# A decoder trunk of eight layer norms in split float32: the shift matmul in float32r, 128-column statistics, and two ScalarE operations of the SwiGLU loop in another order

## The reference

```python
x = layer_norm(alpha * x + 0.5 * swiglu_a(x))
x = layer_norm(alpha * x + mixer_i(x))          # layer 0: windowed attention with sinks, layer 1: NSA
x = layer_norm(alpha * x + cross_attention(x, mem))
x = layer_norm(alpha * x + 0.5 * swiglu_b(x))

def swiglu(x, w_gate, w_up, w_down):            # 1024 -> 2816 -> 1024
    return (silu(x @ w_gate) * (x @ w_up)) @ w_down
def layer_norm(x, g, b):
    mu = mean(x); var = mean((x - mu) ** 2)
    return (x - mu) * rsqrt(var + 1e-5) * g + b
```

## Time and profile before

| what | us |
|---|---|
| median of 3 runs | 2193.94 |
| lowest, highest | 2190.92, 2194.06 |
| the profiled execution, its own time | 2193.49 |
| its span in the profile | 2191.7 |

### The profile page before, as it was taken

How to read it: one execution, slowest core, us unless ns; L and a number is a source line. 1 busy time by engine, 2 the same in 40 slices (tenths; PEclk the granted TensorE clock), 3 DMA queues, 4 the chain that set the end, 5 groups by cost and what they waited for, 6 DMA issues and landing times.

```text
span 2191.7 us, 35422 instructions
## 1 busy us (share of the span) xinstructions
PE 2170.3 (99%) x13654; PEld 1923.6 (88%) x13654; DVE 1334.5 (61%) x2315; ACT 1063.1 (49%) x1919; POOL 778.9 (36%) x573
## 2 busy tenths in 40 slices
PE   9999999999999999999999999999999999999998
PEld 8999998878888989898899999887778888989896
DVE  7656666464436928385766666657655346747475
ACT  5434345563435625354643534467654445535353
POOL 3201116557637030305420111555548555020203
PEclk9999999999999999999999999999999999999999
DMA  4333334213313333233232333320004312322332
GB/s 154 119 97 93 110 113 132 77 46 107 124 39 106 106 96 106 97 109 123 87 117 96 97 106 116 116 80 28 20 11 132 109 50 76 115 98 96 107 101 73
DMA packets 58199, 207.50 MB, mean 95 GB/s; under 512 B 6960, under 2 KB 7088, under 8 KB 57264
## 3 DMA queue, kind: packets, MB, share of 16 engines
q1 hardware_dynamic: 56016, 197.68, 28.3%
q10 hardware_dynamic: 2016, 7.55, 0.9%
HBM read 203.10 MB, written 2.10 MB: 94 GB/s over the span
## 4 chain that ended last, share of the span: by engine, by line
PE 93%; DVE 3%; ACT 1%; POOL 1%; issue 1%; DMA 0%; DVEq 0%; ACTq 0%
PE bank L1748 14%; PE bank L1749 14%; PE bank L1750 14%; PE bank L1959 11%; PE bank L1964 11%; PE bank L1961 11%; PE bank L2160 2%; PE bank L2121 2%; PE bank L2093 1%; PE bank L2094 1%; PE bank L1848 1%; PE bank L1849 1%; PE bank L1850 1%; PE bank L1767 1%; PE bank L1778 1%
## 5 line engine op out<-in xcount | busy, mean ns | idle before, releaser
L612 POOL TENSOR_TENSOR w_lo<-w_raw,w_hi 128x1024 fp32r<-128x1024 f32 (+1 forms) x226 | 530.1, 2353 | 1180.6 <-ACT w_hi L789 1180.5
L1748 PE MATMUL bank<-h_hi,w_hi 128*128 128x512 f32 x960 | 381.3, 397 | 2.5 <-DVE h_lo L1552 1.1
L1749 PE MATMUL bank<-h_lo,w_hi 128*128 128x512 f32 x960 | 374.8, 390 | 0.0
L1750 PE MATMUL bank<-h_hi,w_lo 128*128 128x512 f32 x960 | 374.2, 390 | 0.0
L789 ACT ACTIVATE w_hi<-w_raw 128x1024 fp32r<-128x1024 f32 (+1 forms) x227 | 230.3, 1021 | 128.2 <-PE bank L1750 92.5
L1748 PEld LDWEIGHTS bank<-h_hi,w_hi 128*128 128x128 f32 x960 | 180.5, 188 | 47.7 <-issue 4.7
L1750 PEld LDWEIGHTS bank<-h_hi,w_lo 128*128 128x128 f32 x960 | 180.3, 188 | 38.1
L1749 PEld LDWEIGHTS bank<-h_lo,w_hi 128*128 128x128 f32 x960 | 180.5, 188 | 36.2 <-issue 1.9
L1748 PE MATMUL bank<-x_hi,w_hi 128*128 128x512 f32 x352 | 139.4, 396 | 1.5 <-DVE h_lo L1552 1.5
L1959 PE MATMUL bank<-x_hi,w_hi 128*128 128x256 f32 x864 | 139.8, 284 | 0.2
L1961 PE MATMUL bank<-x_lo,w_hi 128*128 128x256 f32 x864 | 139.0, 283 | 0.0
(11 more groups left out here) (306 smaller groups left out, 5045.9 us busy)
## 6 DMA issues: line engine op xcount, KB each, us to landing
w_raw<-w_dram SPq DMA_DIRECT2D x315, 512.0 KB, 3.5
w_raw<-w_dram SPq DMA_DIRECT2D x64, 448.0 KB, 3.2
f<-mem_dram ACTq DMA_DIRECT2D x5, 1024.0 KB, 5.2
out_dram<-t SPq DMA_DIRECT2D x8, 256.0 KB, 2.2
t<-x_dram SPq DMA_DIRECT2D x2, 512.0 KB, 6.8
f<-cmp_w_dram ACTq DMA_DIRECT2D x1, 1024.0 KB, 5.1
t<-x_dram ACTq DMA_DIRECT2D x2, 256.0 KB, 5.4
t<-x_dram ACTq DMA_DIRECT2D x1, 512.0 KB, 8.1
```

The costliest lines, as they stand in the source:

```text
L612: pool.tensor_tensor(w_lo[:, slot(s), 0:n * P], w_raw[:, s % RAW, 0:n * P], w_hi[:, slot(s), 0:n * P].bitcast(F32), ALU.subtract).then_inc ...
L1748: pe.matmul(dst, w_hi[:, slot(s), w], m_hi[:, k, :], start=k == 0, stop=False)
L1749: pe.matmul(dst, w_hi[:, slot(s), w], m_lo[:, k, :], start=False, stop=False)
L1750: last = pe.matmul(dst, w_lo[:, slot(s), w], m_hi[:, k, :], start=False, stop=k == n - 1)
```

## The change

It does six things. (1) `ones8` is a float32r tile, and `shift` multiplies it with `lead`, a float32r copy of `t[:, 0, :]` that ScalarE makes in the new `lead_round` into `pt[:, 0, :]`, as soon as VectorE has finished chunk 0; a new semaphore `lead_ready` stands between them. (2) In the mixers and cross-attention `shift` is issued after slab 2 instead of slab 1. (3) In norms 0 to 5 the statistics' matmuls have 128 columns (`spread`) instead of one, and the readers take the first column of each 128. (4) `warm(8)` is `warm(5)`. (5) In ScalarE's order in the SwiGLU loop, `pair_round(g.next, 0)` stands ahead of `keep2(g)` instead of behind it. (6) The memset of `ones8` goes through a float32 view.

```diff
@@ -97,6 +97,7 @@
         self.keeps = ln in KEEPS
+        self.spread = P if ln in FILL else 1
 
@@ -363,13 +364,14 @@
         t4 = [ptf[:, 1024 * i:1024 * i + 1024].rearrange("p (k s) -> p k s", k=4) for i in range(2)]
+        lead = pt[:, 0, :]
         comb = {1: (x_hi[:, 0:4, half[1]], x_lo[:, 0:4, half[1]]), 2: (rows4[0], rows4[1]), 3: (rows4[2], rows4[3]),
...
         ones = sb("ones", [P, P])
-        ones8 = sb("ones8", [P, P])
+        ones8 = sb("ones8", [P, P], F32R)
         ident = sb("ident", [P, P])
@@ -417,6 +419,7 @@
         out_free = sem("out_free")
+        lead_ready = sem("lead_ready")
         shift_ready = sem("shift_ready")
@@ -524,6 +527,13 @@
             return snap[g.n % 2][:, i, :]
+
+        def by_token(st, b, i=None):
+
+            each = P // st.spread
+            if i is None:
+                return bank[b][:, 0:NT * each].rearrange("p (i n) -> p i n", n=each)[:, :, 0]
+            return bank[b][:, each * i:each * (i + 1)]
 
@@ -614,7 +624,7 @@
             pool.memset(ones[:], 1.0 / D).then_inc(pool_set, 1)
-            pool.memset(ones8[:], 8.0 / D).then_inc(pool_set, 1)
+            pool.memset(ones8[:].bitcast(F32), 8.0 / D).then_inc(pool_set, 1)
             pool.memset(one, 1.0).then_inc(pool_set, 1)
@@ -927,9 +937,10 @@
                             silu_second(before)
+                        if g.next:
+                            pair_round(g.next, 0)
                         keep2(g)
                         if g.next:
-                            pair_round(g.next, 0)
                             if g is begin:
@@ -953,6 +964,8 @@
                         feed(st.out[part][j] + 3)
+                        if not after and j == 0:
+                            lead_round(st)
                         if after and j == 5:
@@ -964,6 +977,11 @@
                         up_round(after)
+
+            def lead_round(st):
+
+                act.wait_ge(out_free, out_reads(st, len(st.out) - 1, 0))
+                act.activation(lead, t[:, 0, :], ACT.Copy).then_inc(lead_ready, 1)
 
@@ -1002,7 +1020,7 @@
                 act.wait_ge(mean_tok, st.ln + 1)
-                act.activation(msq4, bank[B_SHIFT][:, 0:4], ACT.Square).then_inc(msq_ready, 1)
+                act.activation(msq4, by_token(st, B_SHIFT), ACT.Square).then_inc(msq_ready, 1)
                 act.wait_ge(stat, 2 * st.ln + 1)
@@ -1030,6 +1048,8 @@
                     feed(st.out[0][j] + 3)
+                    if j == 0:
+                        lead_round(st)
                     square_chunk(st, j)
@@ -1315,7 +1335,7 @@
                 dve.wait_ge(msq_ready, st.ln + 1)
-                dve.tensor_tensor(var4, bank[B_VAR][:, 0:4], msq4, ALU.subtract).then_inc(stat, 1)
+                dve.tensor_tensor(var4, by_token(st, B_VAR), msq4, ALU.subtract).then_inc(stat, 1)
                 if st is final:
@@ -1914,13 +1934,13 @@
                 for i in range(NT):
-                    last = pe.matmul(bank[B_SHIFT][:, i:i + 1], total[:, P * i:P * i + P], ones[:, 0:1], start=True,
-                                     stop=True)
+                    last = pe.matmul(by_token(st, B_SHIFT, i), total[:, P * i:P * i + P], ones[:, 0:P // st.spread],
+                                     start=True, stop=True)
                 last.then_inc(mean_tok, 1)
...
                 for i in range(NT):
-                    last = pe.matmul(bank[B_VAR][:, i:i + 1], qsum[:, P * i:P * i + P], ones[:, 0:1], start=True,
-                                     stop=True)
+                    last = pe.matmul(by_token(st, B_VAR, i), qsum[:, P * i:P * i + P], ones[:, 0:P // st.spread],
+                                     start=True, stop=True)
                 last.then_inc(sq_tok, 1)
@@ -1931,7 +1951,7 @@
                 if not st.fill and st is not final:
-                    warm(8)
+                    warm(5)
                 if len(st.fill) > 1:
@@ -1939,15 +1959,15 @@
                 pe.wait_ge(pool_set, 6)
-                pe.wait_ge(out_free, out_reads(st, len(st.out) - 1, 0))
-                pe.matmul(bank[B_SHIFT][:], ones8[:], t[:, 0, :], start=True, stop=True).then_inc(shift_ready, 1)
+                pe.wait_ge(lead_ready, st.ln + 1)
+                pe.matmul(bank[B_SHIFT][:], ones8[:], lead, start=True, stop=True).then_inc(shift_ready, 1)
 
...
                     out_slab(st, part, j, range(begun.get(j, 0), n))
-                    if j == 1 and part == len(st.out) - 1:
+                    if j == (1 if st.kind == "ffn" else 2) and part == len(st.out) - 1:
                         shift(st)
```

## The result

The changed kernel takes 2209.18 us (median of six runs, 2207.78 to 2210.72); the kernel before, run beside it, 2192.27 us (six runs, 2190.30 to 2194.06). The ratio is 1.0078, 95% interval 1.0066 to 1.0090: 16.9 us slower by the medians. The profiled execution took 2208.09 us with a span of 2206.3, so 14.6 more than the profiled execution of before.

The account below looks back on a forecast made before the run. TensorE, busy for 99% of the span, bounds the kernel. Shift -5.4, statistics +0.5, idle matmuls 0, order +13.3 and clock +5.6 sum to +14.0 on 2193.5: 2207.5 us, range 2200.5 to 2211.5.

Parts of the forecast that it names:

- The stalls: At prod5 of each SwiGLU stage's first group, PE waits for keep2's copy, queued behind pair_round: 16.5 us over four stages.
- the resumption: Restart of PE after a wait: 0.10 us for a resumed quarter at prod5; in the mixers within the 0.3 us left.
- the step called weak: Today's small waits early in the four SwiGLU stages, 3.2 us, all come back, making the order's net +13.3 us.
- The clock: Granted clock falls at the four SwiGLU stalls, part of its low time inside them: +5.6 us (0 to +8).
- Rival (a): At the SwiGLU stalls the clock holds or falls too late to cost much: +8.4, 2201.9 us; chance 0.22.
- The shift: Float32r shift at the norms: 0.63 us saved at six, 0.8 at each of two mixers; -5.4 us (-6.0 to -4.5).
- Rival (c): PE waits for `lead` at all eight norms by the copy's 0.61, 4.9 us, while stalls stand: 2212.4 us; chance 0.08.
- The statistics: 128-column instead of one-column statistics matmuls, +0.1 us for each of six norms, taken as +0.5 us (0 to +1.6).
- The fall at norm 6: Clock falls to 0.50 there before the change, losing 1.7 us; five idle matmuls cost 0 (-0.6 to +1.7).

## Why the prediction held, and where it was off

**The stalls: right.** Forecast 4.02, 4.07, 4.02 and 4.38 us, 16.5 together; measured 3.95, 3.99, 4.00 and 4.30, 16.24. The place (prod5 of the first group), the cause (the copy queued behind a rounding that waits for VectorE) and the cure (that one group alone) are shown by the three runs on the order. The forecast's figures include 0.10 each for the resumption and the measured ones do not, so the stalls themselves were put 0.1 us too low in all. The waits of before at prod6 and prod3 are gone behind the stalls, so all of the 3.2 us came back, the step called weak.

**The clock: right in kind, mis-sized.** "0.7 to 1.7 us each, I take 1.4: +5.6 us (0 to +8)". The starts of the products give 8.1, just beyond that range, and filling the stall gives back 7.9 by its trace and 9.1 by the medians. Two things were not foreseen. Hardly any of the low time lay in the stall: in the first two SwiGLU stages the clock fell only when PE was at work again, and the whole 1.7 was lost. And in the last two the fall lasted twice as long: 3.41 us each, less the 0.56 and 0.69 in the stall. The low clock lasted 5.7 and 5.4 us after PE had resumed there, where two to three us were forecast; it cost 2.57 and 2.46, above the 1.7 at which a fall was capped. By the windows that is 1.70 + 1.70 + 2.85 + 2.72 = 9.0; the starts give the smaller 8.1, since rows at the low clock stand 0.86 us apart and not 2 x 0.48. Rival (a), a stall with the clock held, is excluded: that is what the filled stall makes, and it is 8 to 9 us faster; its 2200.08 us are close to the 2201.9 that the rival gave.

**The shift: right.** Forecast -5.4; the trace gives 6 x 0.63 + 2 x 0.6 = 5.0, the run with it alone 4.8. The wait for `lead` in the mixers, with the resumption, was put at 0.3: of the 0.7 for shift and wait 0.23 is the shift, so it is 0.47, of which the trace shows 0.23 as idle time. So 0.6 was saved in each mixer and not 0.8, which is the 0.4 by which the sum was too hopeful. Rival (c), a wait at all eight norms, is excluded; and the move to slab 2 in the mixers and cross-attention earns its 1.1 to 1.8 us.

**The statistics: the code was misread.** The text before the result, in its point (3) of the change and in the prediction, says that norms 0 to 5 get 128 columns. It is the reverse: a matmul has `P // st.spread` columns, and `spread` is P for the norms with fill, so norms 0 to 5 keep one column, and norms 6 and 7 get 128. The term of +0.5 us stood for matmuls that did not change. The changed kernel at norm 0 still has one column:

```profile
362.69 0.95 PE L1937 MATMUL bank<-ones,f 128*128 128x1 f32 x8
```

Read rightly the term would have been 0 to 0.2: two norms, and 128 columns cost nearly as little as one. At norm 6 of the changed kernel:

```profile
1834.01 1.16 PE L1937 MATMUL bank<-ones,f 128*128 128x128 f32 x8 [0.17 <-DVE f L1316]
1835.01 1.06 PE L1942 MATMUL bank<-ones,f 128*128 128x128 f32 x8
1835.90 1.02 PE L1946 MATMUL bank<-f,ones 128*128 128x512 f32 x2
```

The starts are 1.00 and 0.89 us apart; in the kernel with five idle matmuls alone, whose groups have one column, they are 0.92 and 0.89 apart at norm 6. That is 0.08 us for the norm.

**The fall at norm 6** The earlier trace rows is absent in the changed kernel and in the one with the width alone, but also in the one with five idle matmuls and one column, and in the one with the shift alone, which has eight idle matmuls and one column as before; its distance from slab 7 to the first low product is 9.18 us too. The kernel with the order alone has a fall there again, at 1840. So neither the width nor `warm` is needed for it to be absent: it comes and goes, and the 0.5 us that the changed kernel gained there is, as far as these traces show, luck. The prediction did not see that the trace of before has a second fall, 1.71 us at 481 to 485, in the first mixer; the changed kernel has none there, but one of 1.70 at 1475 to 1480. Beyond the shift's 0.6, the stretch from the statistics of norm 0 to those of norm 1 is 1.4 us shorter, the one from norm 4 to norm 5 is 1.6 longer: together they all but cancel.

**The sum.** Forecast +14.0 on the profiled execution, measured +14.6: stalls -0.3, clock +2.5, shift +0.4, statistics -0.5, norm 6 -0.5, start-up -1.2 and the two falls in the mixers +0.2 against the forecast, +0.6 together. That the sum is so close is in part luck: the clock was put 2.5 us too low, and a misread term, the shorter start-up and the fall that stayed away at norm 6 took 2.2 off again. By the medians it is +16.9, since the profiled execution of the changed kernel is 1.1 below its median and that of the kernel before 1.2 above its own.

## What to carry to other kernels

Before an operation is moved ahead of another on an in-order engine, look up when its inputs arrive in the first round of the loop, not only in the steady one: in mid-loop the new order is free, at the start of a stage it puts a copy of 0.4 us behind a wait of 3.7. A stall on TensorE of about 4 us is to be costed at 6 here (an estimate: 16.2 us of stall and 7.9 that filling gave back, over four), since the clock falls at it; where such a wait cannot be avoided, idle matmuls in it gave back 8 to 9 of the 23 to 24 us by which the changed kernel is above its own version with the old order. And a move that helps in one place can be kept out of the one where it hurts by a single condition, as the run with the exception shows.

## What the runs showed of the hardware that was not expected

- Behind stalls of the same length the clock fell at different times: in the second SwiGLU stage at 738.3, over a microsecond after PE had resumed at 737.07, in the third at 1096.7, more than one before PE resumed at 1097.86. The windows of the one sum to 1.7 us of full-speed work, those of the other to 3.4, and the last stage has 3.4 in the changed kernel and 1.7 with the order alone. What decides between the two was not found.
- Falls of 1.7 us also occur at places where no change was made, and not in each kernel: at 7 to 12 (start of the kernel), 481 to 485, 1459 to 1463, 1475 to 1480. Two of them stand just behind a wait of TensorE that is much shorter than the stalls: 1.06 us up to 480.15 in the kernel before, 1.51 up to 1474.93 in the changed one. The times of the kernel before go with them: among its runs those with a mean clock of 0.998 took 2189.1 to 2191.1 us, the one with 0.994 took 2194.4, those between overlap with both. The whole scatter of 5.3 us would be about three such falls; that they make it is not shown, and the fall at norm 6 cost only 0.5. The Trainium skill, "TensorE: Matmul & The Clock Gate", section "The HAM clock gate", says that activity releases the throttle; the traces agree in that the clock came back under steady matmuls each time before the end of the kernel, and the kernel with matmuls in its stalls shows no fall there.
- A plain float32 matmul of one column costs nearly as much as one of 128: 0.10 to 0.12 us an instruction against 0.11 to 0.13. One of 512 columns, two instructions, costs 0.86 us against 0.22 to 0.23 in float32r.
